# The index selector placed between the tiles of the in-projection

## The chip, the cores and the metric

The kernel runs one whole decoder layer on one core of a Trainium2 chip. The metric is the device time of one execution in microseconds (us), taken as the median of several runs. The core has five engines that run side by side and wait for one another through semaphores: PE (TensorE, the matrix products; its weight loads are listed apart as PEld), DVE (VectorE), ACT (ScalarE), POOL (GpSimd), and SP, which here only issues transfers.

## The reference

The layer has two head groups with one input projection and one output projection, then a retrieval FFN. Cut to what the change touches:

```python
h = rms_norm(x) @ w_in                       # q, k, v, z (4 heads of 128 each), a, b, c_q, c_kv (256 each), k_idx (64), w_idx (16)
# group A, gated delta rule: conv + silu + l2 norm of q, k; per head 64-row chunks, (a_mat + eye) inverted
g = -exp(a_log) * softplus(a + dt_bias); beta = sigmoid(b)
# group B, sparse attention
cq = rms_norm(c_q);  q = cq @ w_q_up;  q_idx = (cq @ w_qidx_up)      # 16 index heads of 64
ckv = rms_norm(c_kv); k, v = ckv @ w_kv_up
k_idx = layer_norm(k_idx)
score = sum over 16 heads i of w_idx[i] * relu(q_idx[i] @ k_idx.T)   # causal
_, sel = top_k(score, 128)                                           # per query, topk = T // 4
out = softmax(q @ k[sel].T * scale + bias) @ v[sel]
y = x + concat(o_delta * silu(z), out) @ w_out
# PEER: 8 retrieval heads, 128^2 one-neuron experts, top 16 of each
```

T is 512, in four blocks of 128 queries. Block 0 needs no selection (128 keys at most). So 3 x 16 = 48 index products are made: against 256 keys for block 1, 384 for block 2 and 512 for block 3. The top 128 of a row are found by 16 rounds of "largest eight, then strike them out".

## The kernel before, in words

The program is three stages with a barrier between them; within each, every engine has its own list of instructions.

**in_stage** (to 141 us) makes the in-projection, transposed: 21 tiles of 128 columns of `w_in` against all 512 tokens. Each tile is 24 products 128x512 (8 slices of the depth, each as high by high, low by high and high by low part of a split number; L362, L374, L379). SP loads a tile of `w_in`; ACT makes its high part (`split`, L212), DVE its low part (L283); ACT copies the summed bank out (`store`, L216). Tiles 0 to 11 are q, k, v and go through the convolution (DVE L298 and L301, ACT's Silu L225 and Square L228); for the eight q and k tiles a product with ones (L386) sums the squares, and every second one ACT turns two sums into inverse roots (`roots`, L239 and L241, a table load before each). Then come the four z tiles, four latents, and one tile with index key, gates and index weights (`KI0`).

**mixer_stage** (141 to about 380 us) has these parts in PE's order: a prologue (gates, norms of the latents, bias strip; L1147 to L1162); four heads' own products (`row_sums`, `products`, the transposes at L1265), with two `up_project` (L1227, two fp32 products 128x512 each) of the index queries after each; five levels of the blockwise inverse (L1284, then L1292 and L1294), with index products (`index_dots`, L1246) in levels 1 to 4; u and w (L1315, L1320); eight chunks of the recurrence (L1336, L1347, L1359, L1361) with index products and the q, k, v up-projections between; 16 attention units (L1369, L1378), among which the tail's out-projection and query projection are put. An index product is rectified (L1004) and weighed (L1012) by ACT and added up by POOL (L748); DVE takes the rounds of the selection (`take_best`, L808 and L809) between its own work of levels 5, the chunks and the first units.

A row of the array that holds a product is shown in the trace as rows*columns: `64*128` means 64 rows by 128 columns. An index product has 64 rows (`IDIM`), and uses rows 0 to 63 for an even head and 64 to 127 for an odd one:

```python
rows = slice(IDIM * (i % 2), IDIM * (i % 2) + IDIM)
mm(bank[:, 0:S], up_idx[i // 2][rows, b * P:(b + 1) * P], keys_i[rows, 0:S],
   start=True, stop=True).then_inc(s["dots"], 1)
```

**route_stage and value_layer** (about 380 to 1636 us) are the PEER part, in which products follow one another almost without a gap. POOL there makes a low part of a table's tile (`low`, L1890) and issues a gather of rows (`gather`, L2196) in turn; PE's last product of a tile (L2147) waits for the low part.

## Time and profile before

| | us |
|---|---|
| median of 3 runs | 1640.22 |
| lowest, highest | 1639.07, 1640.68 |
| the profiled execution | 1637.79 |
| its span | 1636.0 |
| busy in it: PE, DVE, ACT, POOL | 1572.3, 1301.8, 701.4, 599.8 |

The span is the time from the first to the last instruction in the profiled execution, and 1.8 us lie around it. Busy time of an engine is no measure of what it holds up: what counts is which engine the others wait for in a stretch.

### The profile page before, as it was taken

How to read it: one execution, taken by the hardware profiler on the slowest of the kernel's cores; microseconds unless marked ns; L12 is line 12 of the kernel's file. 1: busy time of each engine (PE TensorE's matmuls, PEld its weight loads, DVE VectorE, ACT ScalarE, POOL GpSimd, SP SyncE). 2: the span in 40 equal slices, each digit the busy share in tenths (PEclk: the TensorE clock that was granted, in tenths of full speed). 3: DMA queues.
4: the chain of work that ended last, by engine and by line, in shares of the span. 5: the costliest groups of instructions: out<-in, count | busy, mean ns of one | idle time of the engine just before them, and what ended most of it. 6: DMA issues, size and time to landing. Idle time of an engine off the chain costs nothing.

```text
span 1636.0 us, 26769 instructions
## 1 busy us (share of the span) xinstructions
PE 1572.3 (96%) x9253; PEld 1363.4 (83%) x9253; DVE 1301.8 (80%) x2391; ACT 701.4 (43%) x1118; POOL 599.8 (37%) x447
## 2 busy tenths in 40 slices
PE   7998889879999999999999999999999999999997
PEld 5876576558789999999999999998888888888886
DVE  6844568866525989999999999758898989888887
ACT  6474357363432334343444444433333333333334
POOL 3000137155403678787532333223333333322220
PEclk9999999989999999999999999999999999999999
DMA  3321011002243588888799999999999999999995
GB/s 134 113 70 60 2 41 27 26 27 90 91 154 111 164 275 290 269 286 288 258 330 342 348 343 348 346 342 398 385 380 394 382 382 389 387 362 338 367 363 188
DMA packets 149112, 404.47 MB, mean 247 GB/s; under 512 B 14176, under 2 KB 71776, under 8 KB 145568
## 3 DMA queue, kind: packets, MB, share of 16 engines
q1 hardware_dynamic: 108704, 243.93, 43.3%
q0 software_dynamic: 36864, 134.23, 21.6%
q10 hardware_dynamic: 3456, 25.17, 3.8%
q8 instruction: 51, 0.84, 0.2%
q14 instruction: 37, 0.30, 0.0%
HBM read 350.77 MB, written 52.51 MB: 246 GB/s over the span
## 4 chain that ended last, share of the span: by engine, by line
PE 56%; DVE 10%; issue 1%; DMA 1%; ACT 1%; POOL 0%; DVEq 0%; ACTq 0%
PE bank L1614 32%; PE bank L2143 7%; PE bank L2147 7%; PE bank L2144 7%; DVE own_waste L1928 3%; PE bank L2167 3%; DMA h<-u_rows_dram,own_experts 1%; DVE back L1979 1%; DVE rt_num L1950 1%; DVE rt_num L1943 1%; DVE rt_work L1944 1%; DVE rt_pos L1972 0%; DVE rt_cand L1962 0%; PE bank L2128 0%; DVE rt_pos L1969 0%
## 5 line engine op out<-in xcount | busy, mean ns | idle before, releaser
L1614 PE MATMUL bank<-rt_u_parts,rt_w_hi 128*128 128x512 f32 x1536 | 369.2, 389 | 0.0
L2143 PE MATMUL bank<-hi_parts,rt_u_parts 128*128 128x384 f32 x1024 | 350.4, 342 | 0.0
L2144 PE MATMUL bank<-lo_parts,rt_u_parts 128*128 128x384 f32 x1024 | 343.4, 335 | 0.0
L1614 PEld LDWEIGHTS bank<-rt_u_parts,rt_w_hi 128*128 128x128 f32 x1536 | 288.1, 188 | 59.8
L1843 ACT ACTIVATE rt_u_parts<-raw 128x1024 fp32r<-128x1024 f32 x126 | 133.8, 1062 | 336.0 <-PE bank L2147 308.0
L1480 ACT ACTIVATE rt_u_parts<-raw 128x1024 fp32r<-128x1024 f32 x128 | 135.9, 1061 | 321.8 <-PE bank L1614 289.8
L2196 POOL DMA_INDIRECT h<-u_rows_dram,own_experts x128 | 172.6, 1348 | 236.5 <-DVE own_waste L1928 222.6
L2202 POOL DMA_INDIRECT qy<-v_dram,own_experts x128 | 131.5, 1027 | 346.7 <-DVE qy L1554 340.8
L1536 DVE TENSOR_TENSOR rt_u_parts<-raw,rt_u_parts 128x1024 fp32r<-128x1024 f32 x128 | 156.7, 1224 | 68.5 <-ACT rt_u_parts L1480 66.5
L1890 POOL TENSOR_TENSOR rt_u_parts<-raw,rt_u_parts 128x1024 fp32r<-128x1024 f32 x66 | 162.8, 2466 | 122.6 <-ACT rt_u_parts L1843 121.0
L2147 PE MATMUL bank<-hi_parts,rt_u_parts 128*128 128x384 f32 x1024 | 198.4, 334 | 2.0 <-POOL rt_u_parts L1890 2.0
L1614 PE MATMUL bank<-rt_u_parts,rt_w_lo 128*128 128x512 f32 x768 | 194.9, 389 | 0.0
L2144 PEld LDWEIGHTS bank<-lo_parts,rt_u_parts 128*128 128x128 f32 x1024 | 193.4, 189 | 0.0
L2143 PEld LDWEIGHTS bank<-hi_parts,rt_u_parts 128*128 128x128 f32 x1024 | 193.2, 189 | 0.0
L2147 PEld LDWEIGHTS bank<-hi_parts,rt_u_parts 128*128 128x128 f32 x1024 | 179.3, 188 | 2.3 <-POOL rt_u_parts L1890 2.3
L1614 PEld LDWEIGHTS bank<-rt_u_parts,rt_w_lo 128*128 128x128 f32 x768 | 144.1, 188 | 29.9
L1554 DVE SCALAR_TENSOR_TENSOR qy<-qy,own_weights 128x1024 f32<-128x1024 f32 x128 | 163.7, 1279 | 0.1
L1928 DVE SCALAR_TENSOR_TENSOR own_waste<-h,bank 128x1024 bf16<-128x1024 f32 x104 | 126.6, 1217 | 5.2 <-DMA h<-u_rows_dram,own_experts 2.1
L1921 DVE TENSOR_TENSOR rt_u_parts<-raw,rt_u_parts 128x1024 fp32r<-128x1024 f32 x60 | 73.6, 1227 | 33.4 <-ACT rt_u_parts L1843 33.2
L1536 DVE TENSOR_TENSOR rt_w_lo<-rt_w,rt_w_hi 128x384 fp32r<-128x384 f32 x128 | 70.5, 551 | 0.7 <-ACT rt_w_hi L1484 0.7
L480 DVE TENSOR_TENSOR conv_parts<-proj,conv_parts 128x1024 fp32r<-128x1024 f32 x22 | 32.7, 1485 | 48.0 <-ACT conv_parts L432 48.0
L1484 ACT ACTIVATE rt_w_hi<-rt_w 128x384 fp32r<-128x384 f32 x128 | 65.4, 511 | 10.9 <-DVE rt_w L1564 10.8
(361 smaller groups left out, 2338.2 us busy)
## 6 DMA issues: line engine op xcount, KB each, us to landing
raw<-u_dram SPq DMA_DIRECT2D x128, 512.0 KB
raw<-v_dram SPq DMA_DIRECT2D x128, 512.0 KB
active_scratch<-rt_act SPq DMA_DIRECT2D x128, 192.0 KB
gates_scratch<-front ACTq DMA_DIRECT2D x12, 1024.0 KB
gates_scratch<-back ACTq DMA_DIRECT2D x12, 1024.0 KB
front<-gates_scratch SPq DMA_DIRECT2D x8, 1536.0 KB
front<-active_scratch SPq DMA_DIRECT2D x64, 192.0 KB
back<-active_scratch SPq DMA_DIRECT2D x64, 192.0 KB
```

Source lines behind the costliest of these rows:

```text
L1480: nc.scalar.activation(v_hi[:, par, :], raw[:, j, :], ACT.Copy).then_inc(v_high, 1)
L1536: nc.vector.tensor_tensor(out, a, high.bitcast(F32), ALU.subtract).then_inc(done, 1)
L1554: nc.vector.scalar_tensor_tensor(own, ring[:, j, :], w_own[:, bass.ds(e, 1)], own, ALU.mult, ALU.add).then_inc(added, 1)
L1614: return mm(bank_of[b][z][:], left[:, b * P:(b + 1) * P], right[:, halves[z]], start=False, stop=stop)
L1843: a(u_hi[:, j % 2, :], raw[:, j % 4, :], ACT.Copy).then_inc(u_high, 1)
L1890: nc.gpsimd.tensor_tensor(u_lo[:, e % 2, :], raw[:, e % 4, :], u_hi[:, e % 2, :].bitcast(F32), ALU.subtract).then_inc(u_low, 1)
L1928: d.scalar_tensor_tensor(waste[:], ring[:, r, :], 1.0, h_tok[:], ALU.mult, ALU.mult, accum_out=dots[:, bass.ds(k, 1)]).then_inc(dot, 1)
L2143: mm(bank, u_hi[:, j % 2, chunk[c]], hi[:, c, 0:TD], start=c == 0, stop=False)
L2144: mm(bank, u_hi[:, j % 2, chunk[c]], lo[:, c, 0:TD], start=False, stop=False)
L2147: last = mm(bank, u_lo[:, j % 2, chunk[c]], hi[:, c, 0:TD], start=False, stop=c == DC - 1)
L2196: t.nc.gpsimd.indirect_dma_start(out=u_ring[:, k % RING, :], out_offset=None, in_=u_rows, in_offset=bass.IndirectOffsetOnAxis(ap=eidx[:, k ...
L2202: t.nc.gpsimd.indirect_dma_start(out=ring[:, k % RING, :], out_offset=None, in_=v_rows, in_offset=bass.IndirectOffsetOnAxis(ap=eidx[:, k:k ...
```

## The change

The tiles of `w_in` are put in another order: first the tile of index key, gates and index weights (`KI0`), then the two latents of the queries, then the twelve q, k, v tiles, the two latents of keys and values, and the four z tiles, which ACT now stores through Silu. With the latents there early, the whole selector moves into `in_stage`. After each 6 of a tile's 24 products PE calls `between`: in tiles 4 and 5 the transposes, the mean and the sums of squares; in tiles 7 and 8 the eight up-projections of the index queries; after tile 8 the sums for the gates; in tiles 9 to 20 one index product each time, 48 in all (block 1 in tiles 9 to 12, block 2 in 13 to 16, block 3 in 17 to 20). ACT rectifies each; POOL weighs those of blocks 1 and 2 by a `tensor_scalar` that the kernel before doesn't have, ACT those of block 3; POOL adds them up. DVE takes the 16 rounds of block 1 and of block 2 in `IN_BEST`'s steps from tile 14 on. The convolution of a tile comes one tile later than it would by the old rule. `w_qidx_up` (1 MB) and the rest of `constants` (768 KB) are loaded by SP after `w_in[5]` and `w_in[3]`.

`mixer_stage` loses its prologue, the up-projections of the index queries and all index products. The latents of keys and values are normalised in levels 1 and 2, the strip is made in level 1, and of the twelve q, k, v up-projections eight go into levels 2 to 5 (two each) and four into chunks 0 to 3. DVE has the 16 rounds of block 3 left for levels and chunks.

Apart from that, in `route_stage` POOL's last four `low` of the first layer come in a row, with the gathers that stood between them after the last, and four transposes of slots (`turn_slots`) move from the end of a tile's products into their midst.

```diff
+ROW_OF = (KI0, CQ0, CQ0 + 1) + tuple(range(QKV_T)) + (CKV0, CKV0 + 1) + tuple(range(Z0, Z0 + H))
+IN_BEST = {14: (1, 0, 3), 15: (1, 3, 6), 16: (1, 6, 9), 17: (1, 9, 12), 18: (1, 12, 16), 19: (2, 0, 5), 20: (2, 5, 10), 21: (2, 10, 16)}
...
+            def indexer(i, k):
+                if i < DOT_TILE:
+                    take_up(DOTS * (i - UP_TILE) + k)
+                else:
+                    q = DOTS * (i - DOT_TILE) + k
+                    rectify(q)
+                    if of_block(q)[0] == OWN:
+                        weigh(q)
...
+            for i in range(8, NPROJ + 1):
+                if i < NPROJ:
+                    split(i)
+                indexer(i - 1, 0)
                 store(i - 2)
+                indexer(i - 1, 1)
+                if 0 <= i - 9 < QKV_T:
+                    convolved(i - 9)
+                indexer(i - 1, 2)
...
+                if i >= 14 and i % 2 == 0:
+                    roots((i - 14) // 2)
+                indexer(i - 1, 3)
...
+            for q in range(NDOTS):
...
+                if b < OWN:
+                    nc.gpsimd.tensor_scalar(row, row, early.w_idx[:, b, i:i + 1], None, ALU.mult).then_inc(weighed, 1)
...
+                nc.gpsimd.tensor_tensor(score[b][:, 0:S], first[:, 0:S], row, ALU.add).then_inc(score_s, 2 if i == 1 else 1)
...
+            def index_dots(q):
+                b, i = of_block(q)
...
+                if q >= 2:
+                    pe.wait_ge(relu, q - 1)
+                rows = slice(IDIM * (i % 2), IDIM * (i % 2) + IDIM)
+                mm(t.bank[4 + q % 2][:, 0:reach(b)], up_idx[i // 2][rows, b * P:(b + 1) * P], keys_i[rows, 0:reach(b)],
+                   start=True, stop=True).then_inc(dots, 1)
...
+                elif UP_TILE <= i < DOT_TILE:
+                    up_project(DOTS * (i - UP_TILE) + k)
+                elif i >= DOT_TILE:
+                    index_dots(DOTS * (i - DOT_TILE) + k)
...
+                    if made[0] % 6 == 0 and i >= LEAD:
+                        between(i, made[0] // 6 - 1)
...
-    LEVEL_BEST = {(3, 3): (1, 0, 2), (4, 1): (1, 2, 4), (4, 3): (1, 4, 6), (5, 1): (1, 6, 8), (5, 3): (1, 8, 9)}
+    LEVEL_BEST = {(1, 3): (3, 0, 1), (2, 3): (3, 1, 2), (3, 3): (3, 2, 4), (4, 3): (3, 4, 5)}
+    CHUNK_BEST = tuple((3, 5 + n, 6 + n) for n in range(NCH))
...
+                        elif h % 2:
+                            up_project(2 * level - 4 + h // 2)
...
+                    if LEVEL_UPS + n < NUP:
+                        up_project(LEVEL_UPS + n)
...
-                for e in range(BODY + 1, START[1]):
+                for e in range(BODY + 1, START[1] - BRIDGE):
                     low(e)
                     gather(e - BODY)
-                for k in range(START[1] - BODY, EARLY_DOTS + RING):
+                for e in range(START[1] - BRIDGE, START[1]):
+                    low(e)
+                for k in range(START[1] - BRIDGE - BODY, EARLY_DOTS + RING):
                     gather(k)
```

What stands in a row on PE shows the three places. The first is one tile of the in-projection in its second half. Before (a q or k tile; its products by line, then the product with ones, L386):

```order
L362 MATMUL bank<-hi_parts,qy_parts 128x512 [waits in_stored,in_w_high]
L362 MATMUL bank<-hi_parts,qy_parts 128x512 x7
L374 MATMUL bank<-hi_parts,qy_parts 128x512 [waits in_w_low]
L374 MATMUL bank<-hi_parts,qy_parts 128x512 x7
L379 MATMUL bank<-lo_parts,qy_parts 128x512 x8
L386 MATMUL bank<-h,cst 128x512 [waits conv_rooted,conv_squared]
```

After, the tile with number 17, all but its first product (L622 are its 24 products, L584 the index products, the last row L662 the product with ones):

```order
L622 MATMUL bank<-hi_parts,qy_parts 128x512 x5
L584 MATMUL bank<-proj,front 128x512 [waits idx_relu]
L622 MATMUL bank<-hi_parts,qy_parts 128x512 x2
L622 MATMUL bank<-hi_parts,qy_parts 128x512 [waits in_w_low]
L622 MATMUL bank<-hi_parts,qy_parts 128x512 x3
L584 MATMUL bank<-proj,front 128x512 [waits idx_relu]
L622 MATMUL bank<-hi_parts,qy_parts 128x512 x4
L622 MATMUL bank<-lo_parts,qy_parts 128x512 x2
L584 MATMUL bank<-proj,front 128x512 [waits idx_relu]
L622 MATMUL bank<-lo_parts,qy_parts 128x512 x6
L584 MATMUL bank<-proj,front 128x512 [waits idx_relu]
L662 MATMUL bank<-h,cst 128x512 [waits conv_rooted,conv_squared]
```

Four index products of 512 keys now stand singly between products of the other kind; ACT's rectifying of the product two earlier (`idx_relu`) is waited for at each. The second place is one head's turn in the mixer. Before (L1227 are the up-projections):

```order
L1181 MATMUL bank<-cst,conv 128x128 [waits gdn_taken]
L1181 MATMUL bank<-cst,conv 128x128 x7
L1189 MATMUL bank<-conv 64x2x64 [waits gdn_qk]
L1189 MATMUL bank<-conv 64x2x64 x7
L1265 MATMUL bank<-cst,raw 64x64 [waits gdn_at,gdn_a]
L1265 MATMUL bank<-cst,raw 64x64 x7
L1227 MATMUL bank<-proj,hi 128x512 [waits dsa_up_out]
L1227 MATMUL bank<-proj,hi 128x512
L1227 MATMUL bank<-proj,hi 128x512 [waits dsa_up_out]
L1227 MATMUL bank<-proj,hi 128x512
```

After, the same turn, whose lines are now L1284 to L1340:

```order
L1284 MATMUL bank<-lo,cst 128x4x64 [waits gdn_exp3,gdn_gl]
L1284 MATMUL bank<-lo,cst 128x4x64
L1286 MATMUL bank<-lo,cst 128x256
L1287 MATMUL bank<-gate_small,cst 128x256
L1295 MATMUL bank<-cst,conv 128x128 [waits gdn_taken]
L1295 MATMUL bank<-cst,conv 128x128 x7
L1303 MATMUL bank<-conv 64x2x64 [waits gdn_qk]
L1303 MATMUL bank<-conv 64x2x64 x7
L1340 MATMUL bank<-cst,raw 64x64 [waits gdn_at,gdn_a]
L1340 MATMUL bank<-cst,raw 64x64 x7
```

The up-projections are gone from it, and with them the waits for `dsa_up_out`; the transposes (L1265, now L1340) are followed at once by the next head. The third place is the end of a half level of the inverse, before and then after (L1292 and L1294, now L1362 and L1364, are the level's own; L1246 index products; L1326 an up-projection):

```order
L1292 MATMUL bank<-front,qy 64x64 x2
L1294 MATMUL bank<-qy,front 64x64 x2
L1246 MATMUL bank<-proj 128x256 [waits dsa_relu] x4
L1292 MATMUL bank<-front,qy 64x64 [waits gdn_xs]
L1292 MATMUL bank<-front,qy 64x64
```

```order
L1362 MATMUL bank<-front,qy 64x64 x2
L1364 MATMUL bank<-qy,front 64x64 x2
L1326 MATMUL bank<-proj 128x512 [waits dsa_strip_s,dsa_wq]
L1326 MATMUL bank<-proj 128x512
L1362 MATMUL bank<-front,qy 64x64 [waits gdn_xs]
```

Where four index products stood, two products of one up-projection stand now.

## Rows read from the trace of the kernel before

**Rows 1.** Windows: stretch, busy us (and instructions) of PE, PEld, DVE, ACT, POOL; PEclk, DMA share, GB/s

```profile
100.00:120.00 20.00, 17.87 (x73) 13.44 (x72) 5.62 (x8) 17.11 (x19) 0.00 (x0) 1.00 0.21 72
140.00:160.00 20.00, 15.84 (x70) 9.81 (x69) 9.58 (x32) 11.55 (x24) 3.09 (x5) 0.91 0.21 61
260.00:280.00 20.00, 20.00 (x108) 12.11 (x107) 18.32 (x45) 18.10 (x36) 16.79 (x13) 1.00 0.01 2
```

**Rows 2.** Timeline of PE in in_stage: start us, us, line, shapes, count, idle before

```profile
104.32 1.10 PE L386 MATMUL bank<-h,cst 128*128 128x512 f32 x2 [2.13 <-ACT qy L239]
...
110.73 1.02 PE L386 MATMUL bank<-h,cst 128*128 128x512 f32 x2
...
117.07 1.02 PE L386 MATMUL bank<-h,cst 128*128 128x512 f32 x2
```

**Rows 3.** Timeline: PE's first in the mixer, and the first of its heads

```profile
141.72 0.63 PE L1147 MATMUL bank<-cst,proj 128*128 128x128 f32 x4 [0.94 <-PEq L187]
...
151.43 0.80 PE L1170 MATMUL bank<-lo,cst 128*128 128x256 f32 x2 [1.94 <-DVE lo L853]
```

**Rows 4.** Timeline of PE over the heads: two up-projections each, then level 1

```profile
179.05 3.70 PE L1227 MATMUL bank<-proj,hi 128*128 128x512 f32 x8 [0.97 <-ACT proj L994]
...
187.96 3.70 PE L1227 MATMUL bank<-proj,hi 128*128 128x512 f32 x8 [0.97 <-ACT proj L994]
...
194.25 1.95 PE L1284 MATMUL bank<-qy,raw 64*64 64x64 f32 x49 [1.98 <-DVE raw L900]
```

**Rows 5.** Timeline of DVE at the last head

```profile
185.46 0.69 DVE L875 TENSOR_TENSOR qy<-bank,gdn_small 128x512 f32<-128x512 f32 x1 [3.25 <-PE bank L1181]
```

**Rows 6.** Timeline of PE over the levels

```profile
204.59 1.15 PE L1284 MATMUL bank<-qy,raw 64*64 64x64 f32 x32
...
213.49 0.70 PE L1246 MATMUL bank<-proj 64*128 64x256 f32 x4
...
215.56 1.15 PE L1284 MATMUL bank<-qy,raw 64*64 64x64 f32 x32
...
238.33 1.07 PE L1315 MATMUL bank<-conv,qy 64*64 64x128 f32 x16
```

**Rows 7.** Timeline of PE over the chunks

```profile
248.91 1.09 PE L1336 MATMUL bank<-lo,front 128*64 128x128 f32 x8
...
257.60 1.99 PE L1246 MATMUL bank<-proj 64*128 64x512 f32 x8
259.43 0.71 PE L1347 MATMUL bank<-lo,qy 64*128 64x128 f32 x5
...
282.74 1.99 PE L1227 MATMUL bank<-proj 128*128 128x512 f32 x4
284.66 1.16 PE L1347 MATMUL bank<-lo,qy 64*128 64x128 f32 x8
...
290.74 1.99 PE L1227 MATMUL bank<-proj 128*128 128x512 f32 x4
...
310.63 1.94 PE L1227 MATMUL bank<-hi,proj 128*128 128x512 f32 x4
...
313.80 3.60 PE L1389 MATMUL bank<-hi,cst 128*128 128x512 f32 x8
```

**Rows 8.** Groups of ACT from 140 to 380 us, shapes apart: busy us, mean ns

```profile
L1012 ACT ACTIVATE conv<-conv,gdn_w_idx 128x512 f32<-128x512 f32 x16 | 10.7, 733 | 0.0
L1004 ACT ACTIVATE conv<-bank 128x512 f32<-128x512 f32 x16 | 8.7, 600 | 3.3 <-PE bank L1246 3.3
```

**Rows 9.** Groups of POOL from 140 to 380 us, shapes apart

```profile
L748 POOL TENSOR_TENSOR proj<-proj,conv 128x384 f32<-128x384 f32 x12 | 12.3, 1026 | 19.6 <-ACT conv L1012 18.0 <-POOL proj L748 0.5
```

**Rows 10.** Timeline of POOL in in_stage, while DVE works too

```profile
27.24 6.13 POOL L346 TENSOR_TENSOR lo_parts<-proj,hi_parts 128x512 fp32r<-128x512 f32 x4 [26.78 <-ACT hi_parts L221]
```

**Rows 11.** Groups of PE from 780 to 830 us

```profile
L2147 PE MATMUL bank<-hi_parts,rt_u_parts 128*128 128x384 f32 x80 | 15.7, 337 | 2.0 <-POOL rt_u_parts L1890 2.0
L2167 PE MATMUL bank<-qy 128*128 128x128 f16 x67 | 4.6, 220 | 1.2 <-ACT rt_gate L1832 1.2
```

More of the change, by code:

```diff
@@ L179, in in_stage @@
     root, inv = spare[:, 12:14, :], spare[:, 14, :]
-    slots = [proj[:, NPROJ - DC + c, PAD:PAD + T] for c in range(DC)]
+    slots = [proj[:, H + c, PAD:PAD + T] for c in range(DC)]
     v = t.vec
@@ new lines, in rectify, with weigh @@
+            def rectify(q):
+                act.wait_ge(dots, q + 1)
+                if q >= 4:
+                    act.wait_ge(score_s, q - 3)
+                S = reach(of_block(q)[0])
+                f(relu_row(q)[:, 0:S], t.bank[4 + q % 2][:, 0:S], ACT.Relu).then_inc(relu, 1)
+            def weigh(q):
+                b, i = of_block(q)
+                act.wait_ge(relu, q + 1)
+                row = relu_row(q)[:, 0:reach(b)]
+                f(row, row, ACT.Copy, scale=early.w_idx[:, b, i:i + 1]).then_inc(weighed_own, 1)
@@ L293, in convolve @@
             def convolve(j):
[L294 removed]
+                dve.wait_ge(stored, QKV_AT + j + 1)
                 for tap in range(CONV):
@@ L350, in _, with up_project @@
             mm = nc.tensor.matmul
+            ident, ones = t.c(C_ID), t.c(C_ONES)
+            def up_project(n):
+                if n == 0:
+                    pe.wait_ge(wqi_in, 16)
+                    pe.wait_ge(latents, 2)
+                    pe.wait_ge(llog, 2)
+                if n >= 2:
+                    pe.wait_ge(up_out, n - 1)
+                for c in range(2):
+                    last = mm(t.bank[4 + n % 2][:], wqi[:, c, n * P:(n + 1) * P], latent[c], start=c == 0, stop=c == 1)
+                last.then_inc(up, 1)
@@ L351, in _, with product @@
             for i in range(NPROJ):
                 s = i % 2
+                made = [0]
+                def product(left, right):
+                    made[0] += 1
+                    last = mm(bank(i)[:], left, right, start=made[0] == 1, stop=made[0] == 3 * DC)
+                    if made[0] == 3 * DC:
+                        last.then_inc(summed, 1)
+                    if made[0] % 6 == 0 and i >= LEAD:
+                        between(i, made[0] // 6 - 1)
                 pe.wait_ge(w_high, i + 1)
@@ L934, in _ @@
                                  decay, ALU.mult))
-                    for part in range(2):
-                        if part and n < NCH - 1:
-                            dve.wait_ge(s["ds"], n + 1)
-                            tt_(after, dec, t.bank[6][:], ALU.add).then_inc(s["state"], 1)
-                            dve.wait_ge(s["state"], n + 1)
-                        take_best(*CHUNK_BEST[n][part])
+                    if n < NCH - 1:
+                        dve.wait_ge(s["ds"], n + 1)
+                        tt_(after, dec, t.bank[6][:], ALU.add).then_inc(s["state"], 1)
+                        dve.wait_ge(s["state"], n + 1)
+                    take_best(*CHUNK_BEST[n])
                 def logits(u):
@@ L1043, in turn @@
+                for c in range(2):
+                    a(lsq[c], latent[2 + c], ACT.Square).then_inc(s["lsq"], 1)
                 def turn(h):
@@ L1326, in _ @@
                 pe.wait_ge(s["u"], H)
-                for q in range(EARLY, EARLY + 4):
-                    index_dots(q)
                 for n in range(NCH):
@@ L2142, in step @@
                     for c in range(DC):
+                        if phase == 1 and head and j == 3 and c == 2:
+                            pe.wait_ge(s["moved"], 3)
+                            turn_slots(NB - 1, t.bank[4])
                         mm(bank, u_hi[:, j % 2, chunk[c]], hi[:, c, 0:TD], start=c == 0, stop=False)
@@ L2151, in step @@
                         turn_slots(i - 1, t.bank[3])
-                    if phase == 1 and head and j == 3:
-                        pe.wait_ge(s["moved"], 3)
-                        turn_slots(NB - 1, t.bank[4])
-                        pe.wait_ge(s["slots"], NB - 1)
                     if phase == 1:
+                        if head and j == 3:
+                            pe.wait_ge(s["slots"], NB - 1)
                         at = BODY * i + j
```

618 lines of the change are left out of this document (293 added, 325 removed).

## The prediction

> **What bounds the kernel now.** I read the windows first. From 100 to 120 us, in the in-projection, PE is busy in 17.87 of 20 us; from 140 to 160 only in 15.84, at a granted clock of 0.91; from 260 to 280 it is full again, with DVE at 18.32, ACT at 18.10 and POOL at 16.79 beside it [rows 1]. So PE bounds the stage into which the work is moved, and the mixer out of which it is taken is bound by several engines in turn. The timeline of PE in the in-projection shows one tile with its product of ones every 6.34 us (110.73 to 117.07) and at 104.32 one wait of 2.13 us for ACT's roots, which is just what is missing in that window [rows 2]: otherwise there is no free room on PE. In the mixer the prologue holds PE off for 9.71 us (141.72 to 151.43), with small steps that wait for each other [rows 3]. A head takes 8.91 us, of which 3.6 are the two index up-projections (187.96 to the next row's engine time, 3.70 as listed) and 0.97 the wait for ACT to clear a bank [rows 4]; DVE idles 3.25 us of each head, so it works 5.66 [rows 5]. In the chunks PE's products follow one another without a wait [rows 7]. From 380 us on PE is bound by its own products, and nothing of the selector is there.
>
> The question is then how PE's time for the moved products compares before and after, and what the mixer gets back.
>
> **What is added to the in-projection.** Up-projections: four records of 128x512 each. Eight records take 3.43 to 3.6 us [rows 4], 0.43 each; so 1.71 for an up-projection and 13.7 for eight. The four transposes, mean, three sums of squares and the gate sums are priced at four products of 0.86 and about 1.4 for the small ones: 4.8.
>
> Index products: this is the largest term. In the kernel before they come in twos or fours, even and odd head in turn, and eight records of 64x512 take 1.83 us (257.60 to 259.43), 0.229 a record [rows 7], against the 0.43 of a 128-row record with as many columns. I take this as two products that run side by side in the two halves of the rows. What speaks for it are the chunk's products at L1347, also 64\*128, but all in the same half: x8 from 284.66 have 1.16 listed [rows 7], some 0.13 each for 128 columns, where 0.43 scaled to 128 columns is 0.11. A 64-row product with no partner thus costs as much as a full one. After the change each index product stands alone between six products of the projection on either side, so I price it at the full 0.43, 0.64 or 0.86 us (256, 384, 512 keys, two records scaled from 0.43): 16 x 1.93 = 30.9 us.
>
> Each also changes the form of the array from 128\*128 to 64\*128 and back. From 282.74 to 284.66 an up-projection and the change to 64\*128 take 1.92, where four records alone take 1.71 [rows 7]: 0.21 for one change. 48 x 2 x 0.21 = 20.2 us. The bounds: nothing, if the change hides in the long stream of an fp32r product, and 0.25 each way; I take the row. The Trainium skill's "TensorEngine Tiling (Array Packing)" says under Key Properties that changing the tiling mode drains TensorE and that different tiles run in parallel. By it both readings above hold, the 0.21 per change among them; a sum that took the products at the paired rate and the change at nothing would be 35 us lower.
>
> The sum on PE is 13.7 + 4.8 + 30.9 + 20.2 = 69.6. The 2.13 waits for roots [rows 2] stay about as they are, in other tiles: zero. ACT, POOL and DVE follow close behind in the last tiles: 1.5. At the end the last index product must be rectified (0.60), weighed (0.73) [rows 8], added and fenced by POOL before the barrier, where now only a store stands: 3.5 with the waits. The mixer starts 74.6 us later. The moved loads are early and small against a stage in which SP feeds one tile in 6 us: zero; if `w_qidx_up` were late it would hold tile 7, for at most its own few us.
>
> **What the mixer gets back.** Prologue: 9.7 [rows 3].
>
> Heads: 42.8 us from 151.43 to 194.25 [rows 3, 4]. Without up-projections PE needs 8.91 - 3.43 - 0.97 = 4.5 per head, DVE 5.66 [rows 5]; DVE decides: three heads at 5.8, a first one of about 7.2 (nothing to overlap with) and the end of 2.9 from the last transposes to level 1: 27.5. Gain 15.3.
>
> Levels: 44.1 us from 194.25 to 238.33 [rows 4, 6]. Half a level's four index products of 256 keys, with the wait for rectifying, take 2.07 (213.49 to 215.56) [rows 6] and 0.12 to enter; four of them 8.8; four with 384 keys at about 1.0 (paired rate 0.69, changes 0.33) 4.0: 12.8 go. In come eight up-projections at 1.71 + 0.33 = 2.04 (16.3), the sum of squares of the kv latents and the strip (3.2), and 0.9 for the last bank's copy before u and w: +7.6. The four index products after u and w go: -1.5. Together +6.1. Levels don't shrink, they get longer.
>
> Chunks: a pitch of 8.00 (282.74 to 290.74) contains two up-projections of 1.92 [rows 7], so 4.16 remain. After: four chunks with one up-projection, 6.1 each; three with none, where DVE's step between the products (0.7 and a wait) is no longer covered, 5.1; the last 4.1. That is 43.8, against 61.7 from 248.91 to 310.63 [rows 7]: gain 17.9. DVE has one round of 1.5 us in a chunk in place of four or five and won't hold it up. From the last up-projection at 310.63 to the sums at 313.80 [rows 7] 3.2 us pass, of which 1.0 stay: gain 2.2.
>
> The attention units keep their work. In the PEER part, POOL's late low part costs PE 2.0 us and the slots' products wait 1.2 [rows 11]; both are met by the second edit: 3.0, with 1.2 and 3.2 as bounds.
>
> **The sum**: +74.6 - 9.7 - 15.3 + 6.1 - 17.9 - 2.2 - 3.0 = +32.6. It is made against the profiled execution, 1637.8 us, which lies 2.4 below the median of the runs; so 1640.2 + 32.6 gives about 1672 us: slower, by 2%.
>
> **The rivals.**
>
> (a) *The form changes cost nothing.* Speaks for it: the one row that prices them is of fp32 products with idle sequencer time around, not of fp32r ones. But then other engines hold the tiles. ACT's part of four products of 512 keys is 4 x (0.60 + 0.73) = 5.3 [rows 8]; its other work in the tiles with roots is 17.11 us in a window of 20 [rows 1], or 3.15 tiles of 6.34: 5.4 a tile. That makes 10.7 against PE's 11. So in tiles 17 to 20 little is saved, and of the 20.2 about 14 remain: 1658. Chance 20%.
>
> (b) *POOL or DVE becomes the bound of tiles 13 to 19.* POOL adds a product of 384 keys in 1.03 us [rows 9] and now also weighs it, by an operation that no row shows: between 0 and the two-operand row's 1.03, and a wait between; four of them fill 9 to 10.8 us of a tile of 10.6. But four two-operand operations of 128x512 took 6.13 us, 1.53 each, while DVE worked (27.24) [rows 10], against 1.34 alone; and DVE has 5 rounds of the selection per tile there. If both are slowed as there, POOL's tiles take 2 to 4 us longer each, over four or five tiles, 13 us: 1685. The decisive point is a weighing above about 1.2 us. The skill's "GPSIMD Engine Reference" says that POOL shares its SBUF interfaces with VectorE (Specifications) and that a one-input operation runs about at line rate (Engine selection); by the first this case is likelier, by the second the weighing itself is cheap. Chance 15%.
>
> (c) *The other side: not slower.* The index products cost only the paired rate, 0.229 a record at 512 keys, with nothing for the changes, and ACT and POOL keep up because their rows overlap more than I count. Then 48 products cost 16.4 instead of 51.1, and the sum is 1672 - 35 = 1637; it decides where one costs under 0.39 us with its changes (mine: 1.06). Against it speak L1347's rows and ACT's sum. Chance 7%, split between faster and the same.
>
> (d) *The moved work is as forecast, but the mixer gives more back or less*: heads at PE's 4.5 instead of 5.8, chunks at 4.16, or PE's clock at the first head (0.91 over 140 to 160 us [rows 1]), which is spared when the stage starts without a prologue. Each is 2 to 4 us: it lies in my forecast's own range, 1660 to 1684.
>
> **The numbers.** Forecast 58%: 1672. To hold 8 in 10 the range takes in (a) with some room and most of (b): 1648 to 1690. A measurement of this kernel can tell 0.2%, 3.3 us, from no change. Slower holds all of the forecast, (a) and (b), 93 in 100, less one for what I haven't thought of: 92%; the same 3%, faster 5%.
>
> **What the profile after would show.** PE's tiles 9 to 20 with a pitch of about 5.44 plus four singles: 8.8 for 256, 9.7 for 384 and 10.6 for 512 keys, 0.9 more with a product of ones; L584's records at 0.43 for 512 columns, and 0.2 lost before and behind. The mixer's first product near 216; its first level 27.5 after; eight chunks in 44. POOL's `tensor_scalar` at 0.3 to 1 us. I am wrong if a single L584 reads as half a full product, if the tiles of 384 keys are held by POOL (`idx_relu` late because `idx_score` is late), or if the pitch of a head stays above 7.

## The result, and the profile after

The changed kernel takes 1681.27 us (median of 4 runs, 1679.32 to 1682.02), the kernel before 1640.45 us beside it: ratio 1.025, 95% interval 1.0238 to 1.0262. It is slower by 40.8 us, where 32 were forecast; 1681 lies inside the stated range. The profiled execution has a span of 1677.5 us against 1636.0.

The in-projection first. One tile with index products of 512 keys, in the timeline of PE after the change (L584 an index product, L622 the tile's own products, L662 the one with ones):

```profile
176.90 1.10 PE L662 MATMUL bank<-h,cst 128*128 128x512 f32 x2 [1.32 <-ACT qy L285]
177.43 1.96 PE L622 MATMUL bank<-hi_parts,qy_parts 128*128 128x512 f32 x6
179.32 1.12 PE L584 MATMUL bank<-proj,front 64*128 64x512 f32 x2
180.37 1.65 PE L622 MATMUL bank<-hi_parts,qy_parts 128*128 128x512 f32 x6
181.96 1.12 PE L584 MATMUL bank<-proj,front 64*128 64x512 f32 x2
...
188.29 1.13 PE L662 MATMUL bank<-h,cst 128*128 128x512 f32 x2
```

From one index product to the next (179.32 to 181.96) 2.64 us pass, where six products of the projection alone take a quarter of 5.44, 1.36. So one index product of 512 keys costs 1.28: 0.86 for its columns and 0.42 for the changes of form: 0.19 before the projection's next product (180.37 is 1.05 after 179.32), and 0.23 before the next index product, since the six products between (180.37 to 181.96) take 1.59 in place of 1.36. With 256 keys, in the same view:

```profile
85.61 0.70 PE L584 MATMUL bank<-proj,front 64*128 64x256 f32 x2
86.24 1.67 PE L622 MATMUL bank<-hi_parts,qy_parts 128*128 128x512 f32 x6
87.84 0.70 PE L584 MATMUL bank<-proj,front 64*128 64x256 f32 x2
```

2.23 from one to the next, so 0.87 = 0.43 + 0.44. Both prices are those of the prediction. The whole tile, from one product of ones to the next (176.90 to 188.29), takes 11.4 us, and the wait of 1.32 us for ACT's roots ahead of it is PE's longest in the tiles with index products. The next view is PE's first instructions in the mixer and the first row of level 1:

```profile
214.19 1.94 PE L1295 MATMUL bank<-cst,conv 128*128 128x128 f32 x8 [3.82 <-PEq L232]
216.07 1.97 PE L1303 MATMUL bank<-conv 128*64 128x128 f32 x16
...
244.64 1.65 PE L1354 MATMUL bank<-qy,raw 64*64 64x64 f32 x26 [2.02 <-DVE raw L1085]
```

The mixer starts at 214.19, 72.5 us later than before [rows 3], where 74.6 were forecast. But its first products are slow: 1.94 us and 1.97 listed for what takes 1.04 and 1.09 later, because the clock is at half (0.50 from 214 to 218 us). The windows, with the columns of [rows 1], show where else that is so:

```profile
200.00:220.00 20.00, 16.18 (x63) 9.98 (x63) 12.65 (x27) 14.26 (x19) 9.54 (x10) 0.83 0.19 55
...
240.00:260.00 20.00, 15.93 (x343) 13.42 (x343) 13.78 (x32) 7.33 (x13) 0.00 (x0) 0.83 0.02 3
...
320.00:340.00 20.00, 18.31 (x110) 15.68 (x110) 12.42 (x22) 2.57 (x7) 0.00 (x0) 0.80 0.17 53
340.00:360.00 20.00, 18.31 (x72) 15.38 (x72) 6.79 (x15) 3.94 (x8) 3.58 (x5) 0.52 0.00 0
```

PEclk 0.83 with PE at 16.18 of 20, again 0.83 at the start of the levels, 0.80 from 320 and 0.52 from 340 to 360, where the kernel before had 1.00 in its chunks [rows 1]. The chunks in the timeline of PE, first the start of u and w, the first two chunks and the fifth, then the sixth, the start of the seventh, and the sums of squares:

```profile
294.94 1.09 PE L1387 MATMUL bank<-conv,qy 64*64 64x128 f32 x16 [0.78 <-ACT qy L1179]
...
304.05 1.06 PE L1406 MATMUL bank<-lo,front 128*64 128x128 f32 x8 [0.80 <-ACT front L1214]
...
309.92 1.09 PE L1406 MATMUL bank<-lo,front 128*64 128x128 f32 x8
...
327.59 1.09 PE L1406 MATMUL bank<-lo,front 128*64 128x128 f32 x8
329.52 0.71 PE L1414 MATMUL bank<-lo,qy 64*128 64x128 f32 x4 [0.84 <-DVE lo L1118]
```

```profile
332.96 1.97 PE L1406 MATMUL bank<-lo,front 128*64 128x128 f32 x8
335.78 2.07 PE L1414 MATMUL bank<-lo,qy 64*128 64x128 f32 x8 [0.85 <-DVE lo L1118]
...
341.28 1.97 PE L1406 MATMUL bank<-lo,front 128*64 128x128 f32 x8
...
357.11 4.71 PE L1450 MATMUL bank<-hi,cst 128*128 128x512 f32 x8
```

A chunk with an up-projection takes 5.87 us (304.05 to 309.92; forecast 6.1). From the fifth on there is none, PE waits 0.84 us for DVE, and from 331 us each of the same products takes twice as long (1.97 for the 1.09 of L1406): 8.3 us a chunk (332.96 to 341.28), where 5.1 were forecast.

POOL's groups in the in-projection, shapes apart (columns as in [rows 9]):

```profile
L543 POOL TENSOR_SCALAR raw<-raw,gate_w_idx 128x384 f32<-128x384 f32 x16 | 24.3, 1516 | 4.1 <-ACT raw L328 4.1
...
L553 POOL TENSOR_TENSOR proj<-proj,raw 128x384 f32<-128x384 f32 x14 | 16.0, 1144 | 1.2
```

Stage by stage, from the starts on PE in both timelines:

| | before | after | change | forecast |
|---|---|---|---|---|
| start of the mixer | 141.72 | 214.19 | +72.5 | +74.6 |
| prologue | 9.7 | none | -9.7 | -9.7 |
| heads | 42.8 | 30.4 | -12.4 | -15.3 |
| levels | 44.1 | 50.3 | +6.2 | +7.6 |
| u and w | 10.6 | 9.1 | -1.5 | -1.5 |
| chunks, to the sums of squares | 64.9 | 53.1 | -11.8 | -20.1 |
| the sums, and all behind them in the span | | | -1.8 | -3.0 |
| together | | | +41.5 | +32.6 |

The row behind the sums can be split at two places that both kernels have. Up to PE's first product of `route_stage` (L2128 at 500.67 before, L2191 at 543.30 after) the changed kernel gets 0.7 us back. From there to the first of `value_layer` (L1604 at 1101.45, L1665 at 1142.94) it gets 1.1 back, and this is all that the PEER edits give in the profile, where 3.0 were forecast.

### The profile page after: what moved, and what is told of

The parts are those of the page before. It is cut to its first block, busy times and chain, and to the rows that moved or that the text cites. A ratio compares the mean times of both kernels' runs of the same rounds, so it can differ in the third digit from the quotient of the medians.

```text
span 1677.5 us, 26779 instructions
## 1 busy us (share of the span) xinstructions
PE 1616.0 (96%) x9253; PEld 1377.9 (82%) x9253; DVE 1310.0 (78%) x2391; ACT 702.1 (42%) x1090; POOL 656.8 (39%) x479
## 4 chain that ended last, share of the span: by engine, by line
PE 54%; DVE 11%; issue 1%; ACT 0%; DMA 0%; POOL 0%; DVEq 0%; ACTq 0%
PE bank L1675 31%; PE bank L2209 7%; PE bank L2210 7%; PE bank L2213 7%; DVE own_waste L1991 3%; PE bank L2231 3%; DVE back L2042 1%; DVE rt_num L2013 1%; DVE rt_num L2006 1%; DVE rt_work L2007 1%; DVE rt_pos L2035 0%; DVE rt_pos L2032 0%; DVE rt_cand L2025 0%; DMA h<-u_rows_dram,own_experts 0%; PE bank L2191 0%
## 5 line engine op out<-in xcount | busy, mean ns | idle before, releaser
L2266 POOL DMA_INDIRECT qy<-v_dram,own_experts x128 | 136.1, 1063 | 342.1 <-DVE qy L1615 336.2
L2260 POOL DMA_INDIRECT h<-u_rows_dram,own_experts x128 | 177.6, 1387 | 224.1 <-DVE own_waste L1991 209.9
L622 PE MATMUL bank<-hi_parts,qy_parts 128*128 128x512 f32 x272 | 79.5, 426 | 0.8 <-ACT qy_parts L262 0.8
L622 PEld LDWEIGHTS bank<-hi_parts,qy_parts 128*128 128x128 f32 x272 | 48.9, 188 | 30.9 <-issue 21.7
```

The source lines that it names most:

```text
L2260: t.nc.gpsimd.indirect_dma_start(out=u_ring[:, k % RING, :], out_offset=None, in_=u_rows, in_offset=bass.IndirectOffsetOnAxis(ap=eidx[:, k ...
L2266: t.nc.gpsimd.indirect_dma_start(out=ring[:, k % RING, :], out_offset=None, in_=v_rows, in_offset=bass.IndirectOffsetOnAxis(ap=eidx[:, k:k ...
```

## The experiments

Every ratio below is to runs of the kernel before on the same chip; the kernel before differs by up to 3.3 us from chip to chip, so totals are compared by ratios (0.001 is 1.64 us) and stages by the profiles. Three questions were open: whether the chunks lost their 8 us to the clock, whether the price of the index products was the change of form, and whether anything in this design can be mended.

**Fillers in chunks 4 to 7.**

```diff
                     if LEVEL_UPS + n < NUP:
                         up_project(LEVEL_UPS + n)
+                    else:
+                        mm(t.bank[7][:], ones, t.cst[:, 0:T], start=True, stop=True)
                     pe.wait_ge(s["vnew"], n + 1)
```

> The changed kernel with one more fp32 product 128x512 (0.86 us, into a bank that nobody reads) in chunks 4 to 7, where PE has no up-projection and waits 0.84 us for DVE. Theory A (the clock fell because PE waits there): the granted clock stays at 1.00 from 328 to 358 us, the chunks take about 8 us less, total about 1673. Rival B (the clock falls for another reason, or its fall costs nothing): the chunks keep their 8.3 us, or get longer by 0.86 each, total 1681 to 1685.

Measured: ratio 1.0187 (1.017 to 1.0204), 10 us less than the changed kernel's 1.025. The timeline of PE in two of these chunks, and a window over most of the four:

```profile
332.83 1.09 PE L1406 MATMUL bank<-lo,front 128*64 128x128 f32 x8
333.85 1.13 PE L1412 MATMUL bank<-cst 128*128 128x512 f32 x2
334.90 1.16 PE L1416 MATMUL bank<-lo,qy 64*128 64x128 f32 x8
...
337.86 1.09 PE L1406 MATMUL bank<-lo,front 128*64 128x128 f32 x8
```

```profile
328.00:345.00 17.00, 17.00 (x113) 12.88 (x111) 11.54 (x21) 2.54 (x8) 0.00 (x0) 1.00 0.10 40
```

The clock is 1.00 throughout, the wait for DVE is filled by L1412, and a chunk takes 5.03 us (332.83 to 337.86) where it took 8.3. Theory A is shown in this: useless work of 0.86 us made a chunk 3.3 us shorter, because the clock of everything around it no longer fell to half. A filler does two things at once, it takes the wait away and puts more columns through PE. Which of the two keeps the clock up is not shown. The sums of squares start at 347.95 in place of 357.11.

**Eight up-projections in the chunks.**

```diff
-    LEVEL_UPS = 8
+    LEVEL_UPS = 4
...
-                        elif h % 2:
-                            up_project(2 * level - 4 + h // 2)
+                        elif h == 3:
+                            up_project(level - 2)
```

> The changed kernel with four q, k, v up-projections in levels 2 to 5 and eight in the chunks, one each (after: eight and four). By price alone nothing is won: 1.92 us in a chunk in place of 2.04 in a level, and a wait of 0.84 covered in four chunks: 1678. Theory A (the clock falls when PE waits in chunks 4 to 7): the clock stays at 1.00 there as well and 8 us more come back, total about 1670.

Measured: ratio 1.0174 (1.0157 to 1.0191), 12 us under the changed kernel, where price alone would give 3: the useful work does as cover what the filler does. The levels take 43.0 us (244.78 to 287.75) in place of 50.3, and from the first chunk to the sums of squares 47.1 (296.86 to 343.99) in place of 53.1, with four up-projections more in it. The window from 328 to 345 us has the clock at 1.00. Theory A again.

**Index products two by two.**

```diff
-                elif i >= DOT_TILE:
-                    index_dots(DOTS * (i - DOT_TILE) + k)
+                elif i >= DOT_TILE and k % 2:
+                    index_dots(DOTS * (i - DOT_TILE) + k - 1)
+                    index_dots(DOTS * (i - DOT_TILE) + k)
```

> The changed kernel with the index products two by two, after 12 products of the projection each, so that even and odd head stand side by side. Theory P (PE alone bounds the in-projection; two products side by side cost as one, and half the form changes go): 15.4 + 10.1 = 25.5 us less, total about 1656. Rival Q (POOL, which weighs and adds 32 of the 48 and is busy 75 of 80 us from 85 to 165, bounds the tiles as soon as PE gets faster): 4 to 10 us less, total 1671 to 1677.

Measured: ratio 1.0214 (1.0193 to 1.0235); the mixer starts at 208.59, only 5.6 us earlier. PE's timeline where nothing waits:

```profile
86.60 0.70 PE L584 MATMUL bank<-proj,front 64*128 64x256 f32 x4
87.23 1.20 PE L623 MATMUL bank<-hi_parts,qy_parts 128*128 128x512 f32 x4
...
93.80 0.70 PE L584 MATMUL bank<-proj,front 64*128 64x256 f32 x4
```

Two products of 256 keys take the 0.63 us up to the next row (86.60 to 87.23) that one took alone, and a tile takes 7.2 us (86.60 to 93.80) in place of 8.9. So the price of two side by side is that of one, as theory P says. But three times PE waits for the roots, for 3.09, 3.09 and 3.95 us. PE at the first and the third, and then ACT at the third:

```profile
124.89 1.19 PE L663 MATMUL bank<-h,cst 128*128 128x512 f32 x2 [3.09 <-ACT qy L285]
125.42 4.91 PE L623 MATMUL bank<-hi_parts,qy_parts 128*128 128x512 f32 x12
...
135.48 3.31 PE L623 MATMUL bank<-hi_parts,qy_parts 128*128 128x512 f32 x12
...
164.31 1.13 PE L584 MATMUL bank<-proj,front 64*128 64x512 f32 x4
169.40 1.33 PE L663 MATMUL bank<-h,cst 128*128 128x512 f32 x2 [3.95 <-ACT qy L285]
```

```profile
165.47 0.60 ACT L328 ACTIVATE raw<-bank 128x512 f32<-128x512 f32 x1 [0.43 <-PE bank L584]
166.10 0.72 ACT L334 ACTIVATE raw<-raw,gate_w_idx 128x512 f32<-128x512 f32 x1
166.84 1.28 ACT L285 ACT_TABLE_LOAD   x1
168.14 1.11 ACT L285 ACTIVATE qy<-bank,vec 128x1024 f32<-128x1024 f32 x1
```

ACT's list has the roots (L285) behind the rectifying of the tile's third index product. In pairs that one is made only at the end of the tile (164.31); so ACT rectifies at 165.47, loads its table at 166.84, has the roots' first half at 169.25, and PE's product of ones has waited 3.95 us. The clock then falls (0.91 over each of the windows 125 to 145, 145 to 165, 165 to 185 and 185 to 205 us): the twelve products behind the first wait take 4.91 us where the same take 3.31 ten us later.

So the start of the mixer came 5.6 us earlier and not 25.5, and where the missing 20 went can be read. With a fourth wait, of 2.70 us for ACT's rectifying at 196.52, PE waits 12.8 us in these tiles in place of 2.7. The gap before the mixer is 5.4 in place of 3.8. About 8 us are left; four windows of 20 us at 0.91 are 7.2 us of lost clock, by an estimate from these rows. The slow clock behind the waits thus cost nearly as much as the waits. POOL was full too (19.4 of 20 us from 125 to 165), which left rival Q open; the three runs below that relieve POOL bear on it.

**Index products over all rows.** Each gives the sum of two heads, so all scores and what depends on them are other numbers; columns and all other instructions are the same.

```diff
-                rows = slice(IDIM * (i % 2), IDIM * (i % 2) + IDIM)
+                rows = slice(0, P)
```

> The changed kernel with every index product over all 128 rows, so it computes the sum of two heads and not one head's product: the form of the array never changes, the columns and all other work stay. Theory P (a form change costs 0.21 us, PE alone bounds): 20 us less, total about 1661, each product 0.86 for 512 columns and nothing lost around it. Rival Q (POOL bounds next): 4 to 8 us less, about 1675. Rival R (no price of the form, the 0.21 is that of any stranger among the products): no change, 1681.

Measured: ratio 1.0187 (1.017 to 1.0204), 10 us under the changed kernel; the mixer starts at 203.32, 10.9 us earlier. PE's timeline with 256 keys, and the longest wait:

```profile
84.96 0.60 PE L584 MATMUL bank<-proj,front 128*128 128x256 f32 x2
85.20 1.73 PE L622 MATMUL bank<-hi_parts,qy_parts 128*128 128x512 f32 x6
86.77 0.59 PE L584 MATMUL bank<-proj,front 128*128 128x256 f32 x2
```

```profile
166.97 2.05 PE L662 MATMUL bank<-h,cst 128*128 128x512 f32 x2 [4.83 <-ACT qy L285]
```

From one to the next (84.96 to 86.77) are 1.81 us, against 2.23 with 64 rows: 0.42 less, the two form changes of the prediction, and what is left over 1.36 is 0.45, the columns alone. So 48 x 0.42 = 20 us were taken off PE's own work, and nearly half of it came back: PE waits 7.8 us in these tiles in place of 2.7, the gap before the mixer is 4.7 in place of 3.8, and the clock is at 0.91 from 165 to 185 us and at 0.90 from 185 to 205. Rival R is out, and the form's price is shown. PE's waits are all for ACT (L285 and L328), while POOL is busy 19.4 of 20 us from 125 to 165.

**Pairs, ACT weighing all.** The paired kernel, with POOL left with additions only.

```diff
-                    if of_block(q)[0] == OWN:
-                        weigh(q)
+                    weigh(q)
...
-                if b < OWN:
-                    nc.gpsimd.tensor_scalar(row, row, early.w_idx[:, b, i:i + 1], None, ALU.mult).then_inc(weighed, 1)
```

> The changed kernel with the index products two by two, as in the run paired, and ACT weighing all 48 of them, so that POOL has only the additions. Theory Q (POOL's weighing at 1.3 to 1.6 us each held the tiles of blocks 1 and 2 in the paired run): those tiles get faster, and 8 to 14 us more than in the paired run come back, total about 20 us under the changed kernel. Rival S (ACT, busy 13 to 17 of 20 us there, takes POOL's place at once, or DVE's additions to it do): no more than the paired run's 5 us.

Measured: ratio 1.0221 (1.0204 to 1.0239), not faster than the paired run; the mixer starts at 212.07, 3.5 us later. POOL is busy 6 to 9 of 20 us now, and yet the waits for the roots are still there, 3.74, 3.74 and 3.95 us: theory Q falls, which I had held when I wrote this expectation. The first two are longer by 0.65, as ACT now weighs in those tiles too.

**Pairs, the weighing shared.**

```diff
-                    if of_block(q)[0] == OWN:
+                    if of_block(q)[0] == OWN or q % 2 == 0:
                         weigh(q)
...
-                if b < OWN:
+                if b < OWN and q % 2:
                     pool.wait_ge(relu, q + 1)
```

> The paired run, with the weighing of blocks 1 and 2 shared: even products by ACT, odd ones by POOL. In the paired run POOL was full (19.4 of 20 us), with all on ACT the roots came 3.7 us late. Theory U (the tiles are held by whichever of ACT and POOL has more): both have room now, PE waits less than in either, the mixer starts 4 to 8 us earlier than in the paired run (208.6), at 201 to 205, total about 4 to 8 us less than it. Rival V (what holds the tiles is the order on ACT, roots behind a tile's work, however the weighing is shared): starts at 207 or later.

Measured: ratio 1.0208 (1.0191 to 1.0226), start of the mixer at 209.91: theory U falls, and what rival V says came out. POOL is busy 12 to 13 of 20 us from 85 to 165. The first wait for the roots, in PE's timeline, is that of the run in which ACT weighs all, and longer than the 3.09 us with POOL full:

```profile
125.69 1.10 PE L665 MATMUL bank<-h,cst 128*128 128x512 f32 x2 [3.74 <-ACT qy L285]
```

The third wait is 3.95 us in all these runs. It says nothing of POOL, since ACT weighs the products of that tile in each of them.

**Pairs, weighing with two operands.**

```diff
-nc.gpsimd.tensor_scalar(row, row, early.w_idx[:, b, i:i + 1], None, ALU.mult)
+nc.gpsimd.tensor_tensor(row, row, early.w_idx[:, b, i:i + 1].to_broadcast([P, S]), ALU.mult)
```

> The paired run, with POOL's weighing written as a product of two operands (the weight repeated along the row) in place of the operation with a scalar, which took 1.24 us undisturbed for 384 keys against 1.00 for the addition. Theory W (the operation with a scalar is dearer on POOL): 1.00 for 384 keys, 0.72 for 256, and as POOL is full, about 0.25 x 32 = 6 to 8 us less in the tiles of blocks 1 and 2. Rival X (two operands from memory make POOL and DVE slow each other more): the mean stays near 1.5 and nothing is won.

Measured: ratio 1.0192 (1.0176 to 1.0207), the interval overlaps that of the paired run; the mixer starts at 209.69. POOL's group of the weighing, and PE's second wait for the roots:

```profile
L543 POOL TENSOR_TENSOR raw<-raw,gate_w_idx 128x384 f32<-128x384 f32 x16 | 16.7, 1046 | 7.2 <-ACT raw L328 7.2
```

```profile
145.69 2.05 PE L663 MATMUL bank<-h,cst 128*128 128x512 f32 x2 [3.63 <-ACT qy L285]
```

The operation got shorter by a third (1.05 against 1.56 mean in the paired run) and POOL was idle 7.2 us before it. From 125 to 145 us POOL is busy 16.4 us in place of 19.4, and the wait that follows is not shorter than the paired run's 3.09. The mixer doesn't start earlier: theory W is right on the price, and no gain from it is shown.

The three runs take POOL out as the bound. That the order on ACT is the cause is read from the timelines, in which the roots stand behind the late rectifying. It is not shown by a run, since none moved the roots in the list.

**Kept warm.** The run with eight up-projections in the chunks, and fillers before three gaps.

```diff
+            pe.wait_ge(stored, 18)
+            for _ in range(4):
+                mm(t.bank[1][:], ones, t.cst[:, 0:T], start=True, stop=True)
...
+                    if h == H - 1:
+                        for _ in range(4):
+                            mm(t.bank[7][:], ones, t.cst[:, 0:T], start=True, stop=True)
                     pe.wait_ge(s["a"], h + 1)
...
+                for _ in range(2):
+                    mm(t.bank[7][:], ones, t.cst[:, 0:T], start=True, stop=True)
                 pe.wait_ge(s["prep"], H)
```

> The run spread with filler products (0.86 us each, into banks that nobody reads) where PE idles before the mixer (four), before the last head's transposes (four) and before level 1 (two). Theory A (the granted clock falls after PE idles, and the work behind the gap pays for it): the clock stays near 1.00 from 214 to 220 and from 244 to 250 us, and about 5 us less than the run spread. Rival B: the fillers only shift the work behind them, and it is no faster.

Measured: ratio 1.0131 (1.0116 to 1.0147), 7 us less than without the fillers by the ratios and 4.8 by the spans. Windows at the start of the mixer and of the levels:

```profile
214.00:220.00 6.00, 4.89 (x35) 3.20 (x33) 3.85 (x7) 3.21 (x5) 3.10 (x6) 1.00 0.52 156
...
242.00:250.00 8.00, 7.79 (x155) 5.44 (x155) 5.03 (x12) 3.33 (x6) 0.00 (x0) 1.00 0.01 2
```

Both at 1.00, where the changed kernel had 0.50 from 214 to 218 and 0.50 from 244 to 248. The fillers cost 1.0 us at the start of the mixer (215.18) and bring 3.2 by u and w: against the run without them the heads take 28.1 us (215.18 to 243.27) in place of 30.6, and the levels 41.3 (to 284.52) in place of 43.0.

**All repairs**, with ACT weighing all, and then with the weighing shared; both put the edits above together.

> The repairs together: paired products, ACT weighing, eight up-projections in the chunks, fillers. If they add up: 20 + 12 + 5 us under the changed kernel, some 4 us over the kernel before, so still not faster. If ACT bounds the in-projection instead: 15 us over the kernel before.

> The shared weighing with all other repairs (paired products, eight up-projections in the chunks, fillers). If the in-projection gains the 4 to 8 us of theory U over the paired run: some 12 us over the kernel before. If not, 17 us, as with ACT weighing all. Either way slower than before: PE's added 44 us in the in-projection (13.7 up-projections, 4.8, 15.4 products, 10.1 form changes) are more than the mixer gives back.

Measured: ratios 1.0109 (1.0094 to 1.0125) and 1.0114 (1.0098 to 1.0129). The design with every repair tried here is still 18 us slower than the kernel before, where 4 were expected if they add up. They don't: pairing, with the weighing moved, gives 3.6 us on top of the run kept warm, and the intervals overlap. PE's waits of 3.74, 3.74, 3.95 and 2.70 us for ACT in the in-projection stand in both.

**The PEER edits alone**, in the kernel before (their diff stands with the change).

> The kernel before with only the two edits of the PEER part (POOL's four last low parts in a row, the slots' transposes in the midst of a tile). Theory A: PE's waits of 2.0 and 1.2 us go and nothing takes their place: 3 us faster than before. Rival B: the gathers that were moved back delay DVE's dots, and the time stays within 1 us.

Measured: ratio 0.9987 (0.9978 to 0.9996), 2.1 us faster: at the edge of what can be told. PE's waits around the place:

```profile
805.34 1.68 PE L2152 MATMUL bank<-hi_parts,rt_u_parts 128*128 128x384 f32 x8 [1.23 <-DVE rt_u_parts L1923]
807.90 1.05 PE L2170 MATMUL bank<-qy 128*128 128x128 f16 x16 [0.87 <-DVE qy L2055]
```

POOL's 2.0 is gone, but 1.23 for DVE's low part and 0.87 for the slots stand there, where before there were 2.0 and 1.2 [rows 11]: 1.1 us less. From PE's first product of `route_stage` to the first of `value_layer` it takes 599.7 us (500.74 to 1100.40) in place of 600.8, also 1.1. The interval of the times (0.7 to 3.6 us) holds that as well as theory A's 3. That nothing takes the place of the waits is wrong.

**The kernel before, with the PEER edits and fillers.**

```diff
+                mm(t.bank[1][:], ones, t.cst[:, 0:T], start=True, stop=True)
...
+                for _ in range(2):
+                    mm(t.bank[1][:], ones, t.cst[:, 0:T], start=True, stop=True)
                 pe.wait_ge(s["strip_s"], 2)
...
+                    if u == 0 or 2 <= u < 8:
+                        for _ in range(2 if u < 4 else 1):
+                            mm(t.bank[2 if u else 5][:], ones, t.cst[:, 0:T], start=True, stop=True)
                     pe.wait_ge(s["prob"], u + 1)
```

> The kernel before with the two edits of the PEER part and with filler products (0.86 us each, into banks that nobody reads) in the prologue of the mixer (three) and in attention units 0 and 2 to 7 (two each up to unit 3, then one). Theory A (granted clock falls after gaps, the work behind pays): the clock at the first head stays at 1.00, 1.5 to 2 us come back there, 1 to 2 us in the units, on top of the 2.3 us of the PEER edits: 4 to 6 us faster than before. Rival B: in the units DVE bounds, so that fillers there only delay PE's transposes: no faster than the PEER edits alone.

Measured: ratio 0.9983 (0.9973 to 0.9993). The interval overlaps that of the PEER edits alone, so no gain of the fillers is shown. Windows, and the start of level 1:

```profile
151.40:154.00 2.60, 2.48 (x10) 1.52 (x9) 0.60 (x2) 1.89 (x6) 0.00 (x0) 1.00 0.30 25
154.00:156.00 2.00, 2.00 (x23) 1.73 (x23) 0.57 (x1) 1.29 (x3) 0.05 (x1) 1.00 0.00 0
325.00:335.00 10.00, 7.05 (x26) 3.62 (x25) 9.41 (x24) 3.84 (x15) 1.36 (x2) 0.94 0.00 1
```

```profile
193.68 2.39 PE L1287 MATMUL bank<-qy,raw 64*64 64x64 f32 x64 [1.98 <-DVE raw L900]
```

The clock is at 1.00 at the first head, where it was 0.58 and 0.69 before, and 0.94 from 325 to 335 us, where it was 0.50; yet level 1 starts only 0.6 us earlier than before [rows 4], the fillers having delayed the first head by 1.1 us. (The run of the PEER edits alone, with the same code there as before, had 0.50 from 151.4 to 156 us, and its four heads took 45.2 us, from 150.55 to 195.73, against 42.8 before and 41.1 with fillers: this stretch differs by 2 us from one execution to the next, as much as the fillers could bring.) It wouldn't have counted either: at a wait of PE for POOL near 359.5 us the three profiles are level again (359.49, 359.55 and 359.48). In the units DVE is busy 9.41 of 10 us with and without fillers. The slow clock costs nothing there.

## Why the prediction was right, and where it was off

**The price of an index product** (the largest term) was right: 0.43, 0.64, 0.86 for the columns and 0.42 for two form changes, read from the tiles and shown twice over by the runs with pairs (two for the price of one) and with all rows (0.42 less). That changing the tiling mode drains TensorE and tiles of different rows run in parallel (the Trainium skill, "TensorEngine Tiling (Array Packing)", Key Properties) agrees with both.

**The start of the mixer** came 2.1 us earlier than forecast. PE's waits in the stage, with the gap at its end, grew by 3.4 us, where 1.5 and 3.5 were allowed for lag and drain; the rest, some 69 us, is PE's own work, for the 69.6 of the sum.

**The heads** were mis-sized: "three heads at 5.8, a first one of about 7.2" and 2.9 gave 27.5, measured 30.4. The heads' pitch was right (5.93, from 227.30 to 233.23); the first was slow, at a clock of 0.50 from 214 to 218 us. The step that failed is that the sum priced the first head at full clock, and (d) even counted the clock there as "spared when the stage starts without a prologue". Behind the gap of 3.82 us before the mixer, of drain and barrier, it was at half. In the run kept warm the heads take 28.1, so 2.5 of the 2.9 are the clock.

**The levels** came out at +6.2 for +7.6, and that they came so near is in part luck: they hold half clock in level 1, which the forecast did not have and which is worth 1.7 us (41.3 in the run kept warm for 43.0 without its fillers). Without it the forecast would have been 3.1 us too high and not 1.4. What was priced too high is not shown.

**The chunks** hold the error: 43.8 was forecast, 52.0 measured. The step was "three with none, where DVE's step between the products is no longer covered, 5.1". The wait itself was right (0.84, chunks of 5.03 with a filler). What was missing is that the granted clock falls to half, 1.2 GHz, after the first such wait and stays there for 25 us. The runs with fillers and with up-projections as cover both give back 9 us and more.

**The PEER part** gave 1.1 in the profile where 3.0 were forecast. The step "both are met by the second edit" failed: the waits of 2.0 and 1.2 us went, and others of 1.23 for DVE's low part and 0.87 for the slots came.

Together the chunks (8.3), the heads (2.9) and the PEER part (1.9) cost 13.1 us more than forecast; the in-projection (2.1), the levels (1.4) and the stretch from the sums to `route_stage` (0.7) 4.2 less: 8.9, the amount by which the forecast of the span was low. The time lies in the range all the same, but the range was made wide for (a) and (b), and neither of them happened. That it also held a clock that none of the rivals had in the chunks is luck.

**Rival (a)**, form changes for nothing, is out by the tiles' rows. What it said of the tiles held another way: taking 20 us off PE gave back 11, with more waits for ACT and a lower clock behind them.

**Rival (b)**, POOL as the bound, is out for this kernel (in the tiles with index products PE waits only for ACT, 1.32 us at most), though near: POOL was busy 19.42 of 20 us from 140 to 160, with 1.52 us mean for a weighing of 384 keys, above the 1.2 that I had named as the point of decision. That point was too low. The Trainium skill's "GPSIMD Engine Reference" (Engine selection) has one-input operations at about line rate and two-input ones slower; here the operation with a scalar took 1.24 us at its shortest (1.52 mean) for 384 keys, and the product of two operands 0.83 (1.05 mean). The measurement decides: the rule does not hold for this operation.

**Rival (c)**, the other side, would have needed the paired price for single products; the rows of L1347 had spoken against it, rightly.

## What to carry to other kernels

Fill-in work must fit the form of what it is put between: 48 half-height products cost 51 us as singles among full-height ones, of which 20 were form changes and 15 the missing partner. Work taken out of a loop that waits on another engine can cost more than its own time, since the clock of the whole loop may halve once it is gone: leave a little work there, and fill only gaps on the path (in the attention units a filler was worth nothing). Count a wait with the slow clock behind it: in the paired run the second cost nearly as much as the first. And when several engines are near full, look at the order on the next one before its load: three ways to relieve POOL gave nothing, and in the timelines the roots stand behind a late rectifying in ACT's list.

## What the runs showed of the hardware

- Behind one wait of 0.84 us at 328.7, PE's first of note since 304, in the first chunk without an up-projection, the granted clock fell: it was 1.00 until 331, 0.65 from 331 to 334 and 0.50 from 334 to 358 us, in which three more waits of 0.84 to 0.85 lie. With fillers in these waits it was at 1.00 from 328 to 345. The wait of 0.80 before the first chunk was followed by 24 us at 1.00. What tells the two apart no run here shows.
- POOL's operation with a scalar per row takes 1.24 us at its shortest for 128x384, a product of two operands with the scalar repeated along the row 0.83. The means over the stage were 1.52 and 1.05.
- Two 64-row products in different halves of the rows cost 0.63 us for 256 columns, up to the next row of the other form, just what one costs.
